# A decoder block on one core: the second token tile's output projection, norm, query projection and routing run by themselves, and those of the last two tiles run beside its expert retrieval

## The reference

```python
h = rms_norm(x, g[0]) * (1.0 + scale1) + shift1
# mixer: attention and convolution branches, gated, then one projection
g_attn, g_conv = jnp.split(jax.nn.sigmoid(gates), N_BRANCHES, axis=-1)   # gates = h @ w_in[:, last 4096]
y = (g_attn * (attn @ w_attn_o) + g_conv * (u @ w_conv_o)) @ w_out
x = x + gate1 * rms_norm(y, g[1])
h = rms_norm(x, g[2]) * (1.0 + scale2) + shift2
# PEER: 128 experts of 16384 are chosen for each token
q = (h @ w_q).reshape(B, S, PEER_HEADS, 2, PEER_HALF)
#   scores of 2 x 128 sub-keys for each of 8 heads, top 16 of each, top 16 of their sums
pre = jnp.einsum('td,tkd->tk', xc, expert_down[ic]).astype(jnp.float32)
act = jax.nn.gelu(pre, approximate=False) * gc
y = jnp.einsum('tk,tkd->td', act.astype(xc.dtype), expert_up[ic])
x = x + gate2 * rms_norm(y, g[3])
```

## Time and profile before

| | us |
|---|---|
| median of 3 runs | 4298.82 (4296.36 to 4303.76) |
| the profiled execution's own time | 4304.93 |
| its span in the trace | 4303.1 |

### The profile page before, as it was taken

The page is one execution under the profiler, slowest core; times in us unless marked ns, Lnnn a source line. Parts: engine busy times, 40 slices in busy tenths (PEclk is TensorE's granted clock), DMA queues, the critical chain, the costliest instruction groups (busy, mean ns, idle before and its releaser), DMA issues.

```text
span 4303.1 us, 37475 instructions
## 1 busy us (share of the span) xinstructions
PE 2801.0 (65%) x15012; PEld 1610.5 (37%) x15012; DVE 2312.8 (54%) x3585; ACT 541.1 (13%) x1191; POOL 1388.9 (32%) x1109
## 2 busy tenths in 40 slices
PE   3799899889888898899795234344444434434435
PEld 2687788789754444445363001101101101101101
DVE  7399779642654434332235556665466564444442
ACT  2211221200210010101211001001011000000000
POOL 2421211000024433432101455344344354354342
PEclk8899999999998999999897555555555555555555
DMA  8554424798669999998432899999999999999998
GB/s 291 181 177 166 147 95 150 274 373 315 212 230 357 415 375 413 379 413 345 186 130 88 347 405 419 422 421 421 422 420 419 422 421 419 421 419 420 421 422 366
DMA packets 303726, 1413.24 MB, mean 328 GB/s; under 512 B 24384, under 2 KB 24512, under 8 KB 167104
## 3 DMA queue, kind: packets, MB, share of 16 engines
q0 software_dynamic: 152064, 1107.36, 62.6%
q1 hardware_dynamic: 145568, 291.53, 19.2%
q10 hardware_dynamic: 5920, 11.94, 0.7%
HBM read 1403.35 MB, written 7.39 MB: 328 GB/s over the span
## 4 chain that ended last, share of the span: by engine, by line
DMA 42%; PE 36%; DVE 13%; POOL 4%; issue 3%; ACT 2%; SPq 0%; DVEq 0%; ACTq 0%; POOLq 0%
PE psum L616 35%; DMA front<-in_down,back 27%; DMA front<-in_up,back 8%; POOL front L586 4%; DVE front L1594 4%; DMA back<-in_up,back 3%; DVE back L1362 2%; DMA back<-in_ada_w 2%; DMA front<-in_w_in 2%; DVE back L1298 1%; DVE back L1331 1%; ACT back L1123 1%; ACT front L1227 0%; POOL back L586 0%; DVE w_low L1317 0%
## 5 line engine op out<-in xcount | busy, mean ns | idle before, releaser
L616 PE MATMUL psum<-front 128*32 128x512 f32 (+2 forms) x6608 | 1392.9, 656 | 1006.4 <-DMA front<-in_up,back 847.6
L1594 DVE CUSTOM_DVE_ANT_0 front<-front,back 128x2048 f32<-128x2048 f32 x512 | 1171.8, 2292 | 1265.5 <-DMA front<-in_down,back 1119.2
L616 PEld LDWEIGHTS psum<-front 128*128 128x128 f32 (+1 forms) x6608 | 574.6, 160 | 1754.1 <-issue 1406.5
L586 POOL DMA_INDIRECT front<-in_down,back x512 | 609.6, 1191 | 1142.4 <-DVE back L1594 797.8
L616 PE MATMUL psum<-back,front 128*32 128x128 f32 (+3 forms) x4400 | 648.1, 462 | 346.5 <-DMA back<-in_up,back 174.4
L586 POOL DMA_INDIRECT front<-in_up,back x442 | 502.3, 1136 | 869.1 <-PE psum L616 825.7
L616 PEld LDWEIGHTS psum<-back,front 128*32 128x32 f32 (+1 forms) x4400 | 377.8, 169 | 629.6 <-issue 371.1
L564 POOL TENSOR_TENSOR w_low<-front,w_high 128x2048 fp32r<-128x2048 f32 x33 | 154.9, 4695 | 562.4 <-ACT w_high L1011 562.4
L616 PE MATMUL psum<-x_high,w_high 128*128 128x512 f32 x640 | 255.4, 399 | 24.6 <-POOL x_low L570 21.4
L616 PE MATMUL psum<-x_low,w_high 128*128 128x512 f32 x640 | 253.2, 396 | 0.0
L616 PE MATMUL psum<-x_high,w_low 128*128 128x512 f32 x640 | 253.0, 395 | 0.0
(11 more groups left out here) (159 smaller groups left out, 1708.2 us busy)
## 6 DMA issues: line engine op xcount, KB each, us to landing
front<-in_w_in SPq DMA_DIRECT2D x116, 1024.0 KB, 5.3
back<-in_ada_w SPq DMA_DIRECT2D x64, 1024.0 KB, 8.6
front<-in_ada_w POOLq DMA_DIRECT2D x32, 1024.0 KB, 9.5
front<-in_w_out SPq DMA_DIRECT2D x32, 1024.0 KB, 5.3
front<-in_w_q SPq DMA_DIRECT2D x32, 1024.0 KB, 5.5
front<-in_w_conv_o SPq DMA_DIRECT2D x16, 1024.0 KB, 8.0
front<-in_w_attn_o SPq DMA_DIRECT2D x16, 512.0 KB, 15.7
front<-in_down,back POOLq DMA_INDIRECT x512
```

What stands on the lines that cost most here:

```text
L586: nc.gpsimd.indirect_dma_start(out=row_, out_offset=None, in_=table[:, :], in_offset=bass.IndirectOffsetOnAxis(ap=idx4[:, t % 2, c:c + 1], ...
L616: return nc.tensor.matmul(o, a, b, start=start, stop=stop)
L1594: V.tensor_tensor_reduce(d_row[s], d_row[s], h2r, 1.0, 0.0, ALU.mult, ALU.add, pre[:, b // 16 % 2, b % 16:b % 16 + 1]).then_inc(dots_done, 1)
```

## The change

`TAIL` becomes a list of five stages: mix of tile 0, rest of tile 0, mix of tiles 1 to 3, rest of tile 1 alone (128 tokens), rest of tiles 2 and 3 (256 tokens). "Rest" is out, norm section, q and routing. `w_out` (16 MB) and `w_q` (16 MB) are therefore streamed three times in place of two, and `x`'s four loads stay four. `PACE` gets a new table: 106 positions over the 48 mix chunks of tiles 1 to 3 (before: 108), the rest of tile 0's 160 positions over the next 17 chunks, 8 more positions with each q group of tile 1 after the first, and 51 positions over the 34 chunks of the last stage. So tile 1's blocks 0 to 23 run between its own routings, and its blocks 24 to 74 beside the last stage. `WIDE` moves from 160 to 208. The scores of a q group are now issued before the retrieval that is due after its last chunk. Tile 2's routing moves from the retrieval into the last stage (the rule becomes `if t == TT - 1`), tile 3's stays.

```diff
-TAIL = ((0, P), (P, S - P))
+STAGES = (("mix", 0, P), ("rest", 0, P), ("mix", P, S - P), ("rest", P, P), ("rest", 2 * P, S - 2 * P))
+NTH = [sum(k == kind for k, _, _ in STAGES[:c]) for c, (kind, _, _) in enumerate(STAGES)]
+FIRST = 2
...
-WIDE = 160
+WIDE = 208
...
+def tail_groups(c):
+    stage, t0, n = STAGES[c]
+    if stage == "mix":
+        return [(kind, cg, k) for cg in range(4) for kind, k in (("ga", 4), ("gc", 4), ("ao", 2), ("co", 2))]
+    return ([("out", i, 4) for i in range(4)] + [("x", t, 1) for t in range(n // P)]
+            + [(kind, i, k) for i in range(4) for kind, k in (("q", 4), ("sc", 0))])
...
 def block_pace():
-    last = 48 + 16 + TAIL[1][1] // P + 4
-    return [min((i + 1) * (128 + DRAIN) // last, 128 + DRAIN) for i in range(tail_chunks(1))]
+    out = [(i + 1) * 106 // 48 for i in range(48)]
+    out += [106 + (i + 1) * (128 + DRAIN - 106) // 17 for i in range(17)]
+    out += [128 + DRAIN + 8 * i for i in range(4) for _ in range(4)]
+    out += [128 + DRAIN + 24 + 3 * (i + 1) // 2 for i in range(tail_chunks(LAST))]
+    return out
+def reached(chunks):
+    return PACE[chunks - 1 - ALONE] if chunks > ALONE else 0
...
-                        if i == WIDE:
-                            pool.wait_ge(g_done, DONE[1, "sc", 3] + 4)
+                        if i == WIDE:
+                            pool.wait_ge(g_done, TAIL_END)
...
+            def rest(c):
+                (_, t0, n), r = STAGES[c], NTH[c]
...
+                for i in range(4):
+                    def scores():
+                        for m in range(4):
+                            pe.wait_ge(act_took, ATOOK[c, "q", i] + m + 1)
...
+                            ins.then_inc(g_done, 1)
+                    if i == 0:
+                        group(4, 4, hT, plain, t0, n, dve_took, VTOOK[c, "x", n // P - 1], None, scores)
-            tail(0)
-            g3_rows()
-            tail(1)
+            for c, (kind, _, _) in enumerate(STAGES):
+                if c == FIRST:
+                    g3_rows()
+                if kind == "mix":
+                    mix(c)
+                else:
+                    rest(c)
             retrieve(END)
...
-                    if first and t < TT and b % 128 >= 28 and n < 4:
+                    if t == TT - 1 and b % 128 >= 28 and n < 4:
...
                 for i in range(4):
-                    passed(c, 4)
+                    passed(4)
                     dve.wait_ge(act_took, ATOOK[c, "sc", i] + 4)
                     for step in range(6):
-                        route(c, i, step)
+                        route(r, i, step)
```

More of the change, by code:

```diff
@@ L88, in tail_counts @@
     d = a = v = 0
[L89 to L93, removed]
+    for c in range(len(STAGES)):
+        for kind, i, _ in tail_groups(c):
             done[c, kind, i], act[c, kind, i], dve[c, kind, i] = d, a, v
@@ L109, in chunk_ends @@
     out, plain = [], 0
[L110 to L113, removed]
+    for c in range(len(STAGES)):
+        for kind, i, k in tail_groups(c):
             for _ in range(k - 1):
@@ L526, in _ @@
             nc.sync.dma_start(keys[0].rearrange("p k c -> p (k c)"), keysT).then_inc(keys_in, 16)
[L527 to L554, removed]
@@ L874, in chunk_in, with chunk_out @@
                 return s
-            def chunk_out(c):
+            def chunk_out():
                 nonlocal chunk_at
                 chunk_at += 1
[L879 to L905, removed]
-                def squares(buf, count, first, last):
-                    for i in range(count):
-                        ins = mm(ps[:, 6, 0:n], ones, buf[:, i, 0:n], first and i == 0, last and i == count - 1)
-                    return ins
@@ new lines, in chunk_out, with group @@
+                retrieve(reached(chunk_at))
+            def group(chunks, per, src, place, t0, n, free, base, between=None, behind=None):
+                for s in range(chunks):
+                    r = tring[chunk_in()]
+                    for m in range(4):
+                        if s == 0 and free is not None:
+                            pe.wait_ge(free, base + m + 1)
+                        for k in range(per):
+                            ins = mm(ps[:, m, 0:n], r[:, k, m * P:(m + 1) * P], src[:, place(per * s + k), t0:t0 + n],
+                                     s == 0 and k == 0, s == chunks - 1 and k == per - 1)
+                        if s == chunks - 1:
+                            ins.then_inc(g_done, 1)
+                    if s < chunks - 1:
+                        ins.then_inc(t_used, 1)
+                    if s == 0 and between is not None:
+                        between()
+                    if s < chunks - 1 or behind is None:
+                        chunk_out()
+                if behind is not None:
+                    behind()
+                    chunk_out()
@@ L935, in tail, with squares @@
                         modulation_columns(2)
+            def rest(c):
+                (_, t0, n), r = STAGES[c], NTH[c]
+                def squares(buf, count, first, last):
+                    for i in range(count):
+                        ins = mm(ps[:, 6, 0:n], ones, buf[:, i, 0:n], first and i == 0, last and i == count - 1)
+                    return ins
                 for i in range(4):
```

210 lines of the change are left out of this document (127 added, 83 removed).

## The result

The changed kernel takes 4315.67 us (median of 7 runs, 4312.08 to 4320.5), the kernel before 4298.82 us beside it. The ratio is 1.0034, with a 95% interval of 1.0022 to 1.0045: a small loss, clear of noise. I had forecast 4268 us, a gain of 0.7%. The time lies just inside my range of 4230 to 4318, and the direction is wrong.

A forecast was written before the change was run, and what follows sets the result against it. DMA bytes bound most of the kernel; a hole from 2000 to 2405 lost 244 us, against 80 us of added loads. Span 2667 + 1591 + 14 = 4272 against 4303, 31 us less, gave 4268 us; range 4230 to 4318.

The forecast's parts named there:

- Out of tile 1: Tile 1's out stage alone: bound by 81 MB of transfers, 200 us at 404 GB/s, ending at 2055 instead of 2074.
- the three rounds: Tile 1, between its first gather at 2116 and block 24's at 2277: eight dots and a routing each, 53 us apart.
- the end of the stage: Last stage, tiles 2 and 3: bound by DMA at 388 GB/s, ending at 2277 + 367 + 15 + 8 = 2667.
- the first rival: Last stage: PE's clock falls and PE outlasts the gathers; at 0.65 the span is 4360, slower; 12 in 100.
- The second: Rival on tile 1's three rounds: eight dots take 45 us instead of 34.5, the gain is gone, 4303; 15 in 100.
- The third: Rival on the last stage: it runs at 421 instead of 388 GB/s and q's 8 us vanish, 4236; 15 in 100.
- In q [...] I take 8 us in all: Last stage's q: DVE's dots and routing, 35 us plus buffer waits per group against four chunks of 10.8 us, cost 8 us.
- the remaining 670 MB go at 421: After the last stage: the remaining bytes move at 421 GB/s in 1591 us, and the end costs 14 us.
- costs nothing by itself: WIDE at 208: no cost, since the stage passes block 202 and three buffers are in the mix's 388 GB/s.
- the 15 us of the norm section: Last stage's norm section: some 41 us, of which twelve rows fill 30 us; with the next start, 15 us are taken.
- 80 us for 33.6 MB: Whole change: 32 more loads of 1.05 MB cost 80 us at 421 GB/s.
- less what has landed: Last stage's bytes: 51 blocks and 34 chunks, less those already landed, are 136 rows, 143 MB, 367 us at 388.

The follow-up runs named there:

- half the bytes: Changed kernel, each w_out and w_q load cut to its first half: in tile 1's pass 4308.43 us (1.0014), in the last stage 4309.17 us (1.0021).
- half the matmuls: Changed kernel with half of the matmuls of w_out and w_q left out in the last stage, loads kept: 4324.48 us, ratio 1.0044.
- the kernel with solid routings: Kernel before with WIDE = 256 in place of 160 and tile 2's four routings each as one block between two dots: 4365.48 us, ratio 1.0153.
- The run with `WIDE` = 256: Kernel before with WIDE = 256 in place of 160, so three buffers of each kind for 96 blocks more: 4319.69 us, ratio 1.0054.
- a kernel with both routings woven: Changed kernel with tile 2's routings and tile 1's routings two to four split into steps between dots: 4269.44 us, ratio 0.9918.

## Why the prediction was wrong

**Right, by its own points.** Out of tile 1 ended at 2057 (forecast 2055), at 412 GB/s and with PE busy 92 of 150 us: bytes, not PE's 58 us, as I said, and half the bytes ended it 16 us earlier. The start of tile 1's gathers, the three rounds and the end of the stage are within 6 us (the last by luck, see below). The clock did not bound the last stage: 0.92 and 0.91, and half the matmuls gained nothing; the first rival falls. The second does too, since the first eight dots were done 35.9 us after their first gather (forecast 34.5). The third falls as well: the stage ran at 400, 183 and 343 GB/s, not at 421.

**Wrong: "In q [...] I take 8 us in all", and "the remaining 670 MB go at 421".** Both sizes come in the main from one mistake. I laid a routing of 21 us against four chunks' transfers and found it covered on average. But while DVE routes it frees no down buffer, POOL's list stands behind the next down gather, and with it the up gathers behind that. The queue then holds at most six gathers, 15 us at 421 GB/s, less than the block (the last one kept DVE from its dots for 24 us, from 2666.5 to 2690.7). At a boundary of 32 blocks there is a second path that I had not seen: the routing delays the dots that ACT waits for, ACT delays PE, and POOL's list stands behind an up gather (31.8 us). The kernel before had tile 2's routing in steps of a few us between dots, in a stretch at 421 GB/s with five buffers, and the change moved it. I named this move in the text of the change and priced it at 8 us; undoing it gives back 25 us. That such blocks cost 11 us each by their form alone, with three buffers and nothing else beside them, is shown by the kernel with solid routings.

**Also wrong: three buffers up to block 208 "costs nothing by itself".** The up buffers grow only with block 208's up gather, which POOL issues behind the down gather of block 230, so the boundary of 32 blocks at 2786, behind the stage, is still paid with three: 340 GB/s for 60 us, 12 us lost, where I had 421. The run with `WIDE` = 256 gives 19 to 23 us for four boundaries, 5 to 6 us each. In the changed kernel this part is not tried by itself, since the weight ring lies in those buffers.

**Too small: the 15 us of the norm section.** Its hole of 40 us at 183 GB/s loses 21 us against the stage's 388, 6 more than I took. PE's three up blocks before the second norm gave 14 us back, in a kernel with both routings woven.

**The sum.** 17 us of the routings (25 less the 8 in the forecast), 12 of the boundary and 6 of the norm section are 35 of the 48 us between forecast and result (42 between the spans). These are estimates from different traces and can overlap. The rest stays open.

**Bytes.** My account charged 80 us for 33.6 MB. By the halves, doubled, I estimate that they cost about 30 us in the changed kernel, from two differences near the noise. The sum did not show this, because it set a rate of transfers to each stretch and let bytes decide its length, where the length was set by chains and the rate followed. That the stage ended at 2667 as forecast is luck. I wrote "less what has landed" and took nothing off: 51 blocks and 34 chunks are 136 rows, and four chunks of `w_out` had landed before 2277, as my own count of the bytes left has it. The stage had 132 rows, 138 MB, to move, and 138 MB it moved; by my rates it should have ended at 2657, and took 10 us more. For the whole forecast the slip is worth only 2 us, since the same bytes then go at 421.

## What to carry to other kernels

When work is moved beside a transfer-bound stream, look not at whether it fits on average but at its longest unbroken block on the engine that frees the buffers, against the time that the outstanding transfers cover (here a block of 18 to 24 us against 15). Weave it in steps. An in-order list like POOL's, which alternates two kinds of transfers, stops for both when either has no free buffer. And a rate below the peak is an outcome: halve the bytes once, and see whether the time follows, before you price bytes by it.

## What was not expected of the hardware

TensorE's clock was 0.92 and 0.91 in the two long windows of the last stage, where PE was busy 142 of 163 and 157 of 187 us. With half the matmuls and half the bytes left out it was 0.77 and 0.79, so that half the work was not half the time: PE was busy 112.8 of 187 us instead of 156.6 in the changed kernel.
